# Sums of weight blocks by adding transfers on negatives that ScalarE writes, in a two-layer transformer kernel

## The reference

```python
def _swiglu(x, w_gate, w_up, w_down):
    return (jax.nn.silu(x @ w_gate) * (x @ w_up)) @ w_down

x = x + 0.5 * _swiglu(_rmsnorm(x, ffn1_norm[l]), ffn1_w_gate[l], ffn1_w_up[l], ffn1_w_down[l])
```

## Time and profile before

| | us |
|---|---|
| median of 3 runs | 1148.25 |
| fastest and slowest of them | 1147.91, 1637.62 |
| profiled execution | 1147.37 |
| its span | 1145.6 |

### The profile page before, as it was taken

How to read it: one execution, slowest core, us unless ns; L and a number is a source line. 1 busy time by engine, 2 the same in 40 slices (tenths; PEclk the granted TensorE clock), 3 DMA queues, 4 the chain that set the end, 5 groups by cost and what they waited for, 6 DMA issues and landing times.

```text
span 1145.6 us, 15668 instructions
## 1 busy us (share of the span) xinstructions
PE 1137.4 (99%) x5477; PEld 932.3 (81%) x5477; DVE 927.9 (81%) x1434; ACT 615.3 (54%) x789; POOL 211.7 (18%) x413
## 2 busy tenths in 40 slices
PE   9999999999999999999999999999999999999997
PEld 7888888888777888888888888888877788888886
DVE  6878886878987687789788788867898695988895
ACT  6455645457764454455454555454677635454453
POOL 2221230062000012121301221302510000122221
PEclk9999999999999999999999999999999999999999
DMA  8976575795325578756659756647953435886552
GB/s 296 312 265 209 165 232 167 239 263 193 125 75 184 184 233 268 260 164 223 205 194 298 256 175 224 207 154 216 274 164 108 141 136 183 284 283 217 162 196 103
DMA packets 168080, 235.82 MB, mean 206 GB/s; under 512 B 17376, under 2 KB 112848, under 8 KB 168016
## 3 DMA queue, kind: packets, MB, share of 16 engines
q1 hardware_dynamic: 146720, 222.23, 59.0%
q0 software_dynamic: 11008, 8.80, 3.2%
q10 hardware_dynamic: 10288, 4.00, 1.4%
HBM read 221.86 MB, written 1.05 MB: 195 GB/s over the span
## 4 chain that ended last, share of the span: by engine, by line
PE 99%; DVE 1%; issue 0%; ACT 0%; POOLq 0%; POOL 0%; DVEq 0%
PE ps L1645 28%; PE ps L1647 28%; PE ps L1646 28%; PE ps L1778 2%; PE ps L1779 2%; PE ps L1777 2%; PE ps L1903 2%; PE ps L1959 2%; PE ps L1931 2%; PE ps L1695 1%; PE ps L1664 1%; DVE wlo L639 0%; PE ps L1874 0%; PE ps L2082 0%; PE ps L1990 0%; PE ps L1950 0%
## 5 line engine op out<-in xcount | busy, mean ns | idle before, releaser
L639 DVE TENSOR_TENSOR wlo<-raw,whi 128x2048 fp32r<-128x2048 f32 (+2 forms) x195 | 427.5, 2198 | 80.5 <-ACT whi L1347 54.0
L1347 ACT ACTIVATE whi<-raw 128x2048 fp32r<-128x2048 f32 (+2 forms) x195 | 359.2, 1843 | 206.4 <-PE ps L1647 160.2
L1645 PE MATMUL ps<-whi,ht_hi 128*128 128x512 f32 (+1 forms) x1064 | 415.8, 391 | 0.6 <-DVE wlo L639 0.6
L1647 PE MATMUL ps<-whi,ht_lo 128*128 128x512 f32 (+1 forms) x1064 | 411.0, 386 | 0.0
L1646 PE MATMUL ps<-wlo,ht_hi 128*128 128x512 f32 (+1 forms) x1064 | 410.5, 386 | 0.0
L1645 PEld LDWEIGHTS ps<-whi,ht_hi 128*128 128x128 f32 x1064 | 199.9, 188 | 40.9 <-ACT whi L1347 1.0
L1647 PEld LDWEIGHTS ps<-whi,ht_lo 128*128 128x128 f32 x1064 | 199.8, 188 | 40.9
L1646 PEld LDWEIGHTS ps<-wlo,ht_hi 128*128 128x128 f32 x1064 | 200.1, 188 | 38.6
L536 POOL DMA_DIRECT2D act_blocks<-act_blocks x224 | 110.0, 499 | 458.0 <-DVE act_blocks L709 458.0
L1645 PE MATMUL ps<-whi,at_hi 128*128 128x512 f32 x304 | 118.5, 390 | 0.0
L1646 PE MATMUL ps<-wlo,at_hi 128*128 128x512 f32 x304 | 118.3, 389 | 0.0
(11 more groups left out here) (235 smaller groups left out, 1266.9 us busy)
## 6 DMA issues: line engine op xcount, KB each, us to landing
raw<-in_ffn_w_down_dram SPq DMA_DIRECT2D x88, 512.0 KB, 4.4
raw<-in_w_in_dram SPq DMA_DIRECT2D x88, 512.0 KB, 4.6
raw<-in_ffn_w_gate_dram SPq DMA_DIRECT2D x77, 512.0 KB, 4.0
raw<-in_ffn_w_up_dram SPq DMA_DIRECT2D x77, 512.0 KB, 5.0
T_raw<-in_ffn_w_gate_dram SPq DMA_DIRECT2D x16, 512.0 KB, 5.8
T_raw<-in_ffn_w_up_dram SPq DMA_DIRECT2D x16, 512.0 KB, 5.9
raw<-in_w_out_dram SPq DMA_DIRECT2D x16, 512.0 KB, 4.3
raw<-in_ffn_w_gate_dram SPq DMA_DIRECT2D x19, 256.0 KB, 2.9
```

Source lines behind the costliest of these rows:

```text
L639: nc.vector.tensor_tensor(wlo[:, n, 0:w], raw[:, n, 0:w], whi[:, n, 0:w].bitcast(F32), ALU.subtract).then_inc(lo_done, 1)
L1347: nc.scalar.activation(whi[:, n, 0:w], raw[:, n, 0:w], ACT.Copy).then_inc(hi_done, 1)
L1645: nc.tensor.matmul(o, xh, wh, start=start, stop=False)
L1647: return nc.tensor.matmul(o, xl, wh, start=False, stop=stop)
```

## The change

The four sums are no longer made by VectorE. SP loads only two blocks, gate(rows 0) into T1's tile and up(rows 0) into T3's. ScalarE negates them in place (`sum_start`, steps 3 and 4), and GpSimd issues one transfer each that adds the second block from memory onto the tile (`add_part`, 1 MB, with `accum_op=ALU.add`). For T2 ScalarE copies T3 and GpSimd adds gate(rows 0) (step 5), for T4 it negates T2 and GpSimd adds gate(rows 512) (step 6). The rounds of ScalarE move to: T1 in step 5, T3 in step 6, T2 and T4 both in step 7. GpSimd's loop over steps 1 to 7 is written out, and its adding transfer stands behind the step's seven crossing transfers. VectorE's `sum_rest` stays where it was.

```diff
-            def block_sum(l, f, m):
-                ...
-                nc.vector.tensor_tensor(o, a, b, ALU.subtract).then_inc(sum_done, 1)
...
-                    if 4 <= i < 7:
-                        block_sum(l, f, {4: 0, 5: 1, 6: 3}[i])
...
-                    if i == 5:
-                        block_sum(l, f, 2)
...
+            def add_part(l, f, m):
+
+                w, row = ((wu, 0), (wu, 512), (wg, 0), (wg, 512))[m]
+                pool.wait_ge(part_neg[m], l * 2 + f + 1)
+                part = w[ds(l, 1), ds(row, 512), ds(PAIR * FSTEP, 512)].rearrange("a (k p) c -> p (a k) c", p=P)
+                pool.dma_start(sum_raw[SUMS[m]][:, :].rearrange("p (k c) -> p k c", k=4), part, accum_op=ALU.add)\
+                    .then_inc(part_added[m], 16)
...
-                with pool.Fori(1, PAIR) as i:
+                for i in range(1, PAIR):
                     cross_act(pool, l, f, i, BY_POOL, act_crossed_rest)
+                    if 3 <= i < 7:
+                        add_part(l, f, i - 3)
...
+            def sum_start(l, f, m):
+
+                r, name = l * 2 + f, SUMS[m]
+                if m < 2:
+                    eng.wait_ge(part_in[m], (r + 1) * 32)
+                else:
+                    eng.wait_ge(part_added[m - 1], (r + 1) * 16)
+                src = sum_raw[name if m < 2 else SUMS[m - 1]]
+                nc.scalar.activation(sum_raw[name][:, :], src[:, :], ACT.Copy, scale=1.0 if m == 2 else -1.0)\
+                    .then_inc(part_neg[m], 1)
...
-                eng.wait_ge(sum_done, (l * 2 + f) * 4 + m + 1)
+                eng.wait_ge(part_added[m], (l * 2 + f + 1) * 16)
...
-                    if 5 <= i:
-                        sum_round(l, f, {5: 0, 6: 1, 7: 3}[i])
                     if i < PAIR - 1:
                         act_round(l, f, i)
-                    if i == 6:
-                        sum_round(l, f, 2)
+                    if 3 <= i < 7:
+                        sum_start(l, f, i - 3)
+                    if 5 <= i:
+                        sum_round(l, f, i - 5)
+                sum_round(l, f, 3)
...
-                parts = [(n, h) for n in range(4) for h in range(2)]
+                parts = [(n, h) for n in range(2) for h in range(2)]
...
-                    w, row = ((wg, 0), (wu, 0), (wu, 512), (wg, 512))[n]
+                    w, row = ((wg, 0), (wu, 0))[n]
```

More of the change, by code:

```diff
@@ L314, in build @@
         act_crossed_rest = [sem(f"act_crossed_rest{n}") for n in range(3)]
-        part_in = [sem(f"part_in{n}") for n in range(4)]
+        part_in = [sem(f"part_in{n}") for n in range(2)]
+        part_neg = [sem(f"part_neg{n}") for n in range(4)]
+        part_added = [sem(f"part_added{n}") for n in range(4)]
         side_sum = sem("side_sum")
@@ L318, in build @@
         side_l = sem("side_l")
-        sum_done = sem("sum_done")
         sum_h = sem("sum_h")
@@ L1304, in cross @@
                         pool.dma_start(dst.rearrange("p g t c b -> p (g t) (c b)"), src).then_inc(crossed[n], 16)
+            def add_part(l, f, m):
+                wg, wu = ((ffn1_w_gate, ffn1_w_up), (ffn2_w_gate, ffn2_w_up))[f]
+                w, row = ((wu, 0), (wu, 512), (wg, 0), (wg, 512))[m]
[3 more added lines that the diff above has]
+                    .then_inc(part_added[m], 16)
             def ffn(l, f):
                 norm(l * 3 + 2 * f)
-                with pool.Fori(1, PAIR) as i:
+                for i in range(1, PAIR):
                     cross_act(pool, l, f, i, BY_POOL, act_crossed_rest)
+                    if 3 <= i < 7:
+                        add_part(l, f, i - 3)
                 pool.drain()
```

## The result

The kernel after takes 1160.74 us (1159.25 to 1161.13, 4 runs) against 1148.08 us before: 1.011 times, interval 1.009 to 1.013. One of the four runs before took 1637.62 us and isn't in the ratio, which goes by the others. The time is inside the 2% that I called no change and inside my range, but well over the 5 us of loss that I forecast. As a number it lies where rival (c) was (1156 to 1171), though by another path. The profiled span is 1159.0 us against 1145.6.

The account below looks back on a forecast made before the run. TensorE, almost never waiting, was taken to bound the kernel. Copies and adding transfers cost 0, the moved rounding 5 us: 1147.37 became 1152.4, plus 0.9 for the runs' median, so 1153 us, range 1147 to 1165.

Parts of the forecast that it names:

- rival (c): Adding transfers land 13 to 17 us after issue, stalling T4's product and crossings: 1156 to 1171 us, chance 0.15.
- What bounds: TensorE is busy 1137.37 of 1138.70 us; relieving other engines can gain at most 1.9 us.
- The moved rounding: T2's rounding in step 7 shifts ScalarE by 1.83 us; TensorE waits 1.2 us for T4's rest, 5 us over four FFNs.
- The adding transfer: GpSimd's 1 MB transfers: 1.2 us to issue, 10 us to land, at most 6.2 us of all DMA engines; cost 0.
- (d): Adding transfers slow in themselves, 17.5 us and more, holding up crossings and sum_start: over 2% slower, chance 0.13.
- The crossings: In steps 3 to 6, act_round starts 7.9 us behind silu at best, 9.85 us in the busiest step.
- Cost: 0: ScalarE's 16 copies, 1.9 us each, leave 2 us or more of room before TensorE needs slab 20.
- Waits at T4's first matmul and nowhere else: Sign in the pair: TensorE waits for VectorE's T4 rest, four times 1.2 us, and shows no other new wait.
- VectorE less busy by 36.5 us: Sign: removing 16 subtractions of 2.284 us makes VectorE 36.5 us less busy.
- ScalarE up by 30: Sign: ScalarE is 30 us more busy after the change.
- Landings of 8 to 13 us: Sign: adding transfers land in 8 to 13 us, and ScalarE doesn't wait for them.
- Silus 16.32 us apart: Sign: silus of steps 2 to 7 stay 16.32 us apart; otherwise the prediction is wrong.

Follow-up runs that it names:

- experiment 7: Kernel after with sum_start ahead of act_round and the roundings of T3 and T2 both in step 6: 1148.42 us, 1.0004 times the kernel before.
- experiment 1: Kernel before with only ScalarE's rounding of T2 moved from step 6 to step 7, ahead of T4's: 1154.4 us, 1.0053 times the kernel before.
- experiment 2: Kernel after with GpSimd only signalling in place of the 16 adding transfers, sums lacking their second block: 1153.3 us, 1.0045 times the kernel before.
- experiment 3: Kernel after with plain 1 MB transfers in place of the adding ones, sums left out: 1153.03 us, 1.0043 times the kernel before.
- experiment 8: Kernel after with only sum_start moved ahead of act_round, T2's and T4's roundings still in step 7: 1153.33 us, 1.0046 times the kernel before.
- experiment 5: Kernel before with three small extra subtractions ahead of T4's rest on VectorE: 1153.48 us, 1.005 times the kernel before.
- experiment 6: Kernel before with six small extra subtractions ahead of T4's rest on VectorE: 1166.22 us, 1.0156 times the kernel before.
- experiment 10: Kernel before with five extra subtractions ahead of T4's rest on VectorE, one run: span 1159.0 us.
- experiment 9: Kernel after run once more, unchanged, one run: span 1157.1 us.

## Why the prediction was off

**What bounds.** Right: TensorE's list decides, nothing taken from VectorE is worth anything (experiment 7 with all sums moved is level with before), and the only question was which wait appears.

**The moved rounding.** Right in place and size: 1.83 us of shift on ScalarE, predicted wait 1.2 us, measured alone 1.06 us in experiments 1, 2, 3 and 8. VectorE's stretch had no gap, as said.

**The adding transfer.** Issue 1.2 us predicted, 1.36 measured; landing 10 us predicted, 8.8 measured; engines' time 6.2 us each, as worked out from twice the bytes. The Trainium skill (Collectives: The Full Stack, "The bandwidth ceiling") says of collectives that a reducing transfer runs at half the rate of a plain one, since its addition reads two sources. The factor here, for transfers inside one core, agrees: adding costs 6.2 us of the engines, plain 2.9, a factor of 2.1; that the second read is what costs, no run shows by itself. The last transfer was in time in the kernel after, so the late sum of rival (c) didn't occur, nor did (d). Its other half, crossings made late by full engines, did, at landings of 8.8 us and not of 13 to 17; that the measured time lies between 1156 and 1171 is no proof of (c).

**The crossings: the step that failed.** The prediction put "Cost: 0" behind ScalarE's copies. Two things in it failed. It took `act_round`'s start from a kernel whose engines have gaps, at most 9.85 us behind silu; with the engines at 0.97 to 1.00 of a step it is 11 us and more. So slab 20's rounding starts at S + 15.2 (S + 15.6 in the first FFN), later than the S + 12.2 to S + 14.2 of the prediction. And it measured the room against one consumer only, TensorE's need of slab 20 at S + 16.2, of which 1.0 us was left. But step 6's products stand behind slab 20's rest on VectorE, and to keep them on the beat the rounding had to start by about S + 12.6 (S + 16.83 for the products, less 2.2 for the rest and 2.0 for the rounding). Nearly the whole forecast of S + 12.2 to S + 14.2 lay past that point. The crossing of step 6 is 2.5 us late by it; of that, step 7's crossing issues, the two roundings and T4's rest inherit 0.9 us in the second FFN (1.1 us in the first). There is no room left for it, since the moved rounding had already used it. Experiments 2, 3 and 8, which take away the transfers, the adding, and the copy behind `act_round` in turn, each bring the waits back from about 2.15 to 1.06 us. The effect is 1.1 us of wait in each FFN, 4.3 us in all.

**The clock: the term that was missing.** I priced a wait at its own length. Behind waits of 1.8 us and more the clock fell in 9 of 15 cases, for 1.6 us each. In the profile of the kernel after that was twice, 3.2 us. Moved rounding 4.3, crossings 4.3, clock 3.2, around the waits, at the start and between the FFNs about 1.6: together 13.4.

**The checks that I named.** Waits at T4's first matmul and nowhere else: seen, but of 2.0 to 2.5 us. VectorE less busy by 36.5 us: 33.3 seen. ScalarE up by 30: 27.5 seen. Landings of 8 to 13 us: seen, and ScalarE waited for none of them. Silus 16.32 us apart: failed, step 6's is 0.64 us late in the second FFN, and that was the sign of the missing term.

## What to carry to other kernels

Where one engine is saturated, as here, work taken from another is worth nothing, and what counts is the latest point of each list: a piece of 1.8 us that moves into a stretch of back-to-back work is paid in full beyond the room of 0.8 us there (experiments 1 and 5). When lateness is traced, follow every consumer behind the late instruction in the lists of both engines, up to the next place without room, not only the saturated engine's next need. And put a producer's start into an engine's idle time ahead of its next wait: with nothing else changed, the copies ahead of `act_round` instead of behind it took the span from 1159.0 to 1151.7 us (experiment 8), and the roundings put back into step 6 took the rest (experiment 7).

## What the runs showed of the hardware

An adding transfer of 1 MB from memory onto SBUF, in 512 rows of 2 KB, holds GpSimd for 1.36 us (0.79 us plain, experiment 3), takes 6.2 us of the 16 DMA engines against 2.9 us for a plain one, and lands in 8.8 us (8.4 to 9.5) in the kernel after, in 10.2 to 11.4 us (medians) in experiment 7, where it starts 4.2 us earlier in its step. Its queue counts 528 packets for each, against 272: (19456 - 11008)/16 and (15360 - 11008)/16.

A crossing of 16 KB on ScalarE's queue lands in 2.0 us at a DMA share of 0.57, in 2.5 us at 0.72 beside plain transfers, and in 5.6 us at 1.00 beside adding ones (medians, step 5 of the first FFN). At a share of 1.07 (the profile's own figure, which can pass 1) in experiments 7 and 8 it is 5.3 and 5.2 us.

TensorE's clock, at full level from 1.3 to 1140 us in the kernel before, went to its half level for about 3 us behind waits of 2.8 to 3.0 us in four of four cases of experiment 6, behind waits of 2.2 to 2.4 us in two of four cases of experiment 10, and in no case of 1.5 us or less (25 waits for T4's rest in seven profiles). But in experiment 9 one wait of 1.83 us had it and one of 2.80 us had not. What decides between them stays open.
